# Root-mean-square normalisation in the second block: the gain applied in its own pass, and all eight tiles of squares summed by TensorE

## What is computed

```python
def rms_norm_2(x, g, eps=1e-6):
    xf = x.astype(jnp.float32)
    y = xf * lax.rsqrt(jnp.mean(xf * xf, axis=-1, keepdims=True) + eps)
    return (y * g.astype(jnp.float32)).astype(x.dtype)

for i in range(DEPTH):                                                   # DEPTH = 2
    h = x + 0.5 * swiglu_2(rms_norm_2(x, norm_ffn1[i]), ...)             # which = 0
    u = rms_norm_2(h, norm_mix[i])                                       # which = 1
    ...                                   # u @ w_in, attention, convolution, gates, w_o
    h = h + 0.5 * swiglu_2(rms_norm_2(h, norm_ffn2[i]), ...)             # which = 2
    x = h + (p[i] @ w_pe_proj[i]) * sigmoid(rms_norm_2(h, norm_pe[i]) @ w_pe_gate[i])   # which = 3
```

## Time and profile before

| | |
|---|---|
| median of 3 runs | 2408.21 us (2407.85 to 2410.92) |
| the profiled execution, its own time | 2407.85 us |
| its span in the trace | 2406.0 us |
| TensorE (PE) busy | 2281.4 us, 95% |
| VectorE (DVE) busy | 1648.2 us, 69% |
| ScalarE (ACT) busy | 1174.0 us, 49% |
| GpSimd (POOL) busy | 183.2 us, 8% |

### The profile page before, as it was taken

One profiled execution on the slowest core, in us unless ns is written; L12 is line 12 of the kernel. 1 busy time (PEld: TensorE's weight loads), 2 busy tenths in 40 slices (PEclk: granted clock), 3 DMA queues, 4 the chain that ended last, 5 costly groups with the idle time before them and its releaser, 6 DMA issues.

```text
span 2406.0 us, 40710 instructions
## 1 busy us (share of the span) xinstructions
PE 2281.4 (95%) x16812; PEld 2151.2 (89%) x16812; DVE 1648.2 (69%) x1717; ACT 1174.0 (49%) x1198; POOL 183.2 (8%) x185
## 2 busy tenths in 40 slices
PE   4999889999999998999899999999999999999999
PEld 4997788799889877899799997899999999889999
DVE  5886786786589876855655569865565546986555
ACT  2443555454354445454354455555355536465534
POOL 0110000010001100000012000012001200001200
PEclk9999999999999999999999999999999999999999
DMA  8996433576569752555545542445544554334453
GB/s 343 350 353 223 152 140 110 211 302 260 192 231 355 304 201 88 187 199 175 183 172 178 183 165 108 140 175 178 189 180 157 182 185 158 112 138 181 182 180 140
DMA packets 75937, 471.55 MB, mean 196 GB/s; under 512 B 8707, under 2 KB 8963, under 8 KB 27580
## 3 DMA queue, kind: packets, MB, share of 16 engines
q1 hardware_dynamic: 53136, 383.80, 43.6%
q0 software_dynamic: 18976, 68.71, 7.6%
q10 hardware_dynamic: 3724, 17.56, 2.0%
HBM read 468.97 MB, written 1.06 MB: 195 GB/s over the span
## 4 chain that ended last, share of the span: by engine, by line
PE 75%; DVE 12%; ACT 6%; DMA 4%; issue 2%; ACTq 0%; DVEq 0%; SPq 0%
PE ab L1736 48%; PE acc L1736 13%; PE acc L1856 8%; DVE wlo L964 3%; ACT whi L417 2%; DMA raw<-stream 2%; DVE sc L1559 1%; PE mb L2078 1%; DMA modmem<-mods 1%; DMA par<-params 1%; PE mb L1907 1%; DVE sc L1049 1%; DVE rstd L1161 1%; DVE x L1159 1%; DVE sc L1157 1%
## 5 line engine op out<-in xcount | busy, mean ns | idle before, releaser
L1736 PE MATMUL ab<-u_hi,whi 128*128 128x256 f32 x3664 | 1051.3, 287 | 33.8 <-DVE wlo L964 11.5
L964 DVE TENSOR_TENSOR wlo<-raw,whi 128x2048 fp32r<-128x2048 f32 x361 | 825.0, 2287 | 320.0 <-ACT whi L417 318.2
L1736 PE MATMUL ab<-u_lo,whi 128*128 128x256 f32 x3664 | 1042.3, 284 | 0.0
L1736 PE MATMUL ab<-u_hi,wlo 128*128 128x256 f32 x3664 | 1041.9, 284 | 0.0
L417 ACT ACTIVATE whi<-raw 128x2048 fp32r<-128x2048 f32 x361 | 688.9, 1910 | 536.7 <-DMA raw<-stream 339.2
L1736 PEld LDWEIGHTS ab<-u_hi,whi 128*128 128x128 f32 x3664 | 708.8, 193 | 49.7 <-issue 30.7
L1736 PEld LDWEIGHTS ab<-u_lo,whi 128*128 128x128 f32 x3664 | 709.1, 194 | 0.4
L1736 PEld LDWEIGHTS ab<-u_hi,wlo 128*128 128x128 f32 x3664 | 708.7, 193 | 0.0
L1736 PE MATMUL acc<-h_hi,whi 128*128 128x256 f32 (+1 forms) x1032 | 293.4, 284 | 6.9 <-DVE sc L1620 3.5
L1736 PE MATMUL acc<-h_lo,whi 128*128 128x256 f32 (+1 forms) x1032 | 292.0, 283 | 0.0
L1736 PE MATMUL acc<-h_hi,wlo 128*128 128x256 f32 (+1 forms) x1032 | 292.0, 283 | 0.0
(11 more groups left out here) (319 smaller groups left out, 2004.1 us busy)
## 6 DMA issues: line engine op xcount, KB each, us to landing
raw<-stream SPq DMA_DIRECT2D x365, 1024.0 KB, 4.8
modmem<-mods POOLq DMA_DIRECT2D x128, 512.0 KB, 6.1
sc<-lnrows ACTq DMA_DIRECT2D x5, 1024.0 KB, 4.9
sc<-start ACTq DMA_DIRECT2D x4, 1024.0 KB, 16.6
gateb<-gaterows ACTq DMA_DIRECT2D x6, 512.0 KB, 4.1
hank<-toep POOLq DMA_DIRECT2D x8, 192.0 KB, 4.0
x<-xT ACTq DMA_DIRECT2D x1, 1024.0 KB, 31.6
x<-xn ACTq DMA_DIRECT2D x1, 1024.0 KB, 5.0
```

Source lines behind the costliest of these rows:

```text
L964: nc.vector.tensor_tensor(wlo[:, n % RAW, :], raw[:, n % RAW, :], whi[:, n % RAW, :].bitcast(F32), ALU.subtract).then_inc(lo_ready, 1)
L1736: ins = nc.tensor.matmul(out, l, r, start=first and i == 0, stop=last and i == 2, skip_group_check=True)
```

## The change

It is made in `norm2` and `squares` only.
- ScalarE now writes x times gain in float32 into tiles `UF` to `UF+7` of `sc` (two instructions for each pair, semaphore `xg_ready`), and then `u_hi` from there by one copy of the pair (`lead`, which waits for `xg_ready`). For `which` 1 to 3 the copy of a pair follows its gain at once; for `which` 0 it follows the gain of the next pair. The four squares come after the last copy.
- ScalarE's `catch_up` stands ahead of pair 1 for `which` 1 to 3, ahead of everything for (1,0), and there is none for (0,0). In the code before it stood behind the first `lead` in all joins but (0,0).
- VectorE makes `u_lo` by `u_lo_pairs`, one subtraction for each pair. `sum_squares` is gone, with its semaphore.
- TensorE's `squares` takes all 8 tiles of squares, with a wait for `sq_ready` for each pair, by 8 float32 matmuls in place of 2.

```diff
@@ scalar: norm2
                 def lead(q):
+                    act.wait_ge(xg_ready, cnt["uf"] + q + 1)
+                    nc.scalar.activation(u_hi[:, 2 * q:2 * q + 2, :], sc[:, UF + 2 * q:UF + 2 * q + 2, :],
+                                         ACT.Copy).then_inc(uhi_ready, 1)
+
+                if (l, which) == (1, 0):
+                    catch_up()
+                for q in range(4):
+                    if which and q == 1:
+                        catch_up()
                     act.wait_ge(x_ready, cnt["x"] + q + 1)
                     for m in (2 * q, 2 * q + 1):
-                        ins = nc.scalar.activation(u_hi[:, m, :], x[:, m, :], ACT.Copy, scale=par[:, gc + m:gc + m + 1])
-                    ins.then_inc(uhi_ready, 1)
-
-                def square(q):
+                        ins = nc.scalar.activation(sc[:, UF + m, :], x[:, m, :], ACT.Copy,
+                                                   scale=par[:, gc + m:gc + m + 1])
+                    ins.then_inc(xg_ready, 1)
+                    if which:
+                        lead(q)
+                    elif q:
+                        lead(q - 1)
+                if not which:
+                    lead(3)
+                cnt["uf"] += 4
+                cnt["x"] += 4
+                for q in range(4):
                     nc.scalar.activation(sc[:, Z + 2 * q:Z + 2 * q + 2, :], x[:, 2 * q:2 * q + 2, :],
                                          ACT.Square).then_inc(sq_ready, 1)
-
-                lead(0)
-                if (l, which) != (0, 0):
-                    catch_up()
-                lead(1)
-                square(0)
-                square(1)
-                lead(2)
-                square(2)
-                lead(3)
-                square(3)
-                cnt["x"] += 4
                 cnt["var"] += 1
@@ vector: norm2
-                def rest(q):
-                    cnt["uhi"] += 1
-                    dve.wait_ge(uhi_ready, cnt["uhi"])
-                    for m in (2 * q, 2 * q + 1):
-                        ins = nc.vector.scalar_tensor_tensor(out=u_lo[:, m, :], in0=x[:, m, :], scalar=par[:, gc + m:gc + m + 1],
-                                                             in1=u_hi[:, m, :].bitcast(F32), op0=ALU.mult, op1=ALU.subtract)
-                    ins.then_inc(u_ready, 1)
-
-                def sum_squares(q):
-                    dve.wait_ge(sq_ready, cnt["sq"] + q + 1)
-                    ins = nc.vector.tensor_tensor(sc[:, Z:Z + 2, :], sc[:, Z:Z + 2, :], sc[:, Z + 2 * q:Z + 2 * q + 2, :], ALU.add)
-                    ...
-                update(0)
-                if which:
-                    rest(0)
-                    update(1)
-                    catch_up()
-                    rest(1)
-                    update(2)
-                    rest(2)
-                    update(3)
-                    sum_squares(1)
-                    sum_squares(2)
-                    rest(3)
-                else:
-                    ...
-                sum_squares(3)
+                for q in range(4):
                     if scale is not None:
                         x_update(q, scale, add)
+                    if which and q == 1:
+                        catch_up()
+                    if which:
+                        u_lo_pairs(q)
+                    elif q:
+                        u_lo_pairs(q - 1)
+                if not which:
+                    u_lo_pairs(3)
                     if scale is not None:
                         catch_up()
@@ tensor
+            def sums(src, tiles, ready, base, out, per=2, done=None):
+
+                for m in range(tiles):
+                    pe.wait_ge(ready, base + m // per + 1)
+                    ins = nc.tensor.matmul(out, meanones, src[:, m, :], start=(m == 0), stop=(m == tiles - 1))
+                ins.then_inc(done, 1)
+
             def squares():
 
-                cnt["sq"] += 1
-                pe.wait_ge(sqsum_ready, cnt["sq"])
-                for m in range(2):
-                    ins = nc.tensor.matmul(mb[:, 1, 0:T], meanones, sc[:, Z + m, :], start=(m == 0), stop=(m == 1))
-                ins.then_inc(var_ready, 1)
+                sums(sc[:, Z:Z + 8, :], DM, sq_ready, cnt["sq"], mb[:, 1, 0:T], 2, var_ready)
+                cnt["sq"] += 4
```

More of the change, by code:

```diff
@@ L218, in build @@
         sq_ready = sem("sq_ready")
-        sqsum_ready = sem("sqsum_ready")
         var_ready = sem("var_ready")
@@ L224, in build @@
         x_ready = sem("x_ready")
+        xg_ready = sem("xg_ready")
         rinv_ready = sem("rinv_ready")
@@ L951, in _ @@
             ph = [0]
-            cnt = {"std": 0, "uhi": 0, "sq": 0, "h": 0, "hhi": 0, "g2": 0, "sig": 0, "row": 0, "gate0": 0, "gate1": 0}
+            cnt = {"std": 0, "uhi": 0, "h": 0, "hhi": 0, "g2": 0, "sig": 0, "row": 0, "gate0": 0, "gate1": 0}
             def link(ins):
@@ L1210, in norm2 @@
             def norm2(l, which, scale=None, add=None):
-                gc = AT["norms2"][0] + 16 * which + 8 * l
-                def update(q):
+                for q in range(4):
                     if scale is not None:
                         x_update(q, scale, add)
-                def rest(q):
-                    cnt["uhi"] += 1
-                    dve.wait_ge(uhi_ready, cnt["uhi"])
-                    for m in (2 * q, 2 * q + 1):
-                        ins = nc.vector.scalar_tensor_tensor(out=u_lo[:, m, :], in0=x[:, m, :], scalar=par[:, gc + m:gc + m + 1],
-                                                             in1=u_hi[:, m, :].bitcast(F32), op0=ALU.mult, op1=ALU.subtract)
-                    ins.then_inc(u_ready, 1)
-                def sum_squares(q):
-                    dve.wait_ge(sq_ready, cnt["sq"] + q + 1)
-                    ins = nc.vector.tensor_tensor(sc[:, Z:Z + 2, :], sc[:, Z:Z + 2, :], sc[:, Z + 2 * q:Z + 2 * q + 2, :], ALU.add)
-                    if q < 3:
-                        link(ins)
-                    else:
-                        ins.then_inc(sqsum_ready, 1)
-                update(0)
-                if which:
-                    rest(0)
-                    update(1)
-                    catch_up()
-                    rest(1)
-                    update(2)
-                    rest(2)
-                    update(3)
-                    sum_squares(1)
-                    sum_squares(2)
-                    rest(3)
[L1246 to L1253, removed]
+                    if which and q == 1:
[6 more added lines that the diff above has]
+                    u_lo_pairs(3)
                     if scale is not None:
                         catch_up()
-                    sum_squares(1)
-                    sum_squares(2)
-                sum_squares(3)
-                cnt["sq"] += 4
                 cnt["std"] += 1
```

## The result

The changed kernel is slower: a median of 2440.20 us (2436.96 to 2441.81, 4 runs) against 2408.03 us (2406.84 to 2410.92, 4 runs), ratio 1.013 with a 95% interval of 1.0112 to 1.0148. The forecast had been 2434, 2427 to 2439: the direction was right, the size 6 us short and just outside the range. The profiled execution took 2437.39 us (span 2435.6), 29.5 more than that of before. So of the 6 us 3.4 show in the trace, and 2.8 are the distance from the profiled execution to the median.

A forecast was written before the change was run, and what follows sets the result against it. PE was taken as the bound, busy for 95% of the span and carrying 75% of the chain that ended last. 20.7 + 4.8 - 0.2 + 0.9 = +26.2 us on 2407.85 gave 2434 us, range 2427 to 2439.

The forecast's parts named there:

- Twelve more records, 2.59 us a join, all on PE's path: PE's squares in all eight joins: 16 records instead of 4, 0.216 us each, nothing hidden, +20.7 us in all.
- The last pair late by 0.8 us in six joins: Ordinary joins: PE stalls for pair 3's u_lo before its first block's last 12 matmuls, 0.8 us each, +4.8 us.
- The squares no wait, the removed sums worth nothing: In (0,1), ScalarE's squares end at 1398.0, PE arrives at 1398.1; VectorE's saved 3 x 0.69 us a join gains nothing.
- (0,0), 2.4: Join (0,0): one 0.69 us subtraction replaces two L1222 (0.88 us) before PE starts, -0.2 us beside the 2.59 of passes.
- (1,0), "I take +0.9 us": Join (1,0): allowance beyond the passes, since PE idles more and the clock may fall again; +0.9 us, bounds 0 and +4.5.
- about 0.65 us that the half clock cost the next block isn't lost: Behind squares in (1,0): the next block no longer runs at half clock, so about 0.65 us is taken back.
- Downstream: After squares: later waits and PE's next block move together with the last record; nothing given back, nothing more lost.
- "Nothing more is lost" downstream: After the joins: no further time added; the attention stretches were forecast at 0 in both layers.
- VectorE as the bound: Rival for the joins: VectorE's savings give 22.6 us back and hide PE's passes, 2385 us; chance 2%.
- cheap passes: Rival for squares: a record costs only 0.12 us, first term 11.5 us, total 2425; chance 3%.
- absorption downstream: Rival: PE's later waits for VectorE's convolution taps absorb the (.,1) joins' extra 3.4 us in each layer, 2427; chance 7%.
- The slower clock: Rival: in (1,0) or at a new stall, one or two more 1.2 GHz stretches on dense work, 2437 to 2442; chance 12%.

The follow-up runs named there:

- TensorE's part alone: Kernel before with squares summing all 8 tiles by 8 float32 matmuls and VectorE's sums gone, u_hi and u_lo made as before: 2424.49 us, ratio 1.0071.
- the first trace: First profiled execution of the changed kernel, set against the first profiled execution of the kernel before: 2437.39 us.
- the other two: Second and third traces of the changed kernel, run again unaltered: second with a median of 2436.14 us (4 runs), third 2436.90 us.
- The second comparison: Changed kernel, unaltered, timed against the kernel before on another occasion: median 2436.14 us (4 runs), ratio 1.0115.
- the first two experiments: Kernel before with 8 float32 matmuls and no VectorE sums: 2424.49 us; kernel before with one more VectorE addition and 1 matmul for 2: 2406.71 us.

## Why the prediction was right, and where it failed

- **Twelve more records, 2.59 us a join, all on PE's path:** shown. TensorE's part alone costs 2.59 in each ordinary join, 2424.49 us in all against 2425 expected, and halving the records gives 0.43 back.
- **The last pair late by 0.8 us in six joins:** shown. PE's new distance is 0.70 to 0.86 us in the first trace (0.67 to 0.98 in the other two), 12 matmuls ahead of squares, and the joins cost 0.67 to 0.83 beyond the passes; the sum is 20.05 us against 20.3 forecast. The chain of gain, copy and subtraction, read from the kernel's start, fitted to 0.1 us.
- **The squares no wait, the removed sums worth nothing:** both as forecast, L1924 having no idle time.
- **(0,0), 2.4:** measured 2.26, 2.57 and 2.44.
- **(1,0), "I take +0.9 us":** this term failed, in two parts. The three starts were right, and so was the statement that the clock might fall. But 5.76 us came in place of 3.5. First, the half clock: the forecast put 0.9 on top of its path, a mean over "may fall", where three traces have it fall each time, at 2.4 to 2.6 us, 2.3 of it ahead of squares. Second, "about 0.65 us that the half clock cost the next block isn't lost": PE waits there for VectorE's weight remainder and the path costs 3.2 at full clock, not 2.56. The forecast's "Downstream" had said itself that nothing is given back. The rows to see the first part by were there. After 1.21 busy us of 3.40 the clock had fallen in this very join, and the forecast's own path had PE idle for the first 3.8 us, then at work for 1.4 of every 3.5. The Trainium skill ("TensorE: Matmul & The Clock Gate", HAM oscillation) describes the same for short groups of matmuls between waits for DMA: after each wait the next group starts at the low level. The trace agrees in kind, for waits on VectorE, with 0.50 granted on all of the 13.7 us.
- **"Nothing more is lost" downstream:** 1.9 us were counted in the attention stretches. The kernel before shows 1.0 of it between two of its own executions, so part of it may be the reference and not the change. This stays open.
- **What the parts add up to** in the joins of the first trace: passes 17.5, the late pair 4.5, the order of the copies in (1,0) with its half clock 6.3, (0,0) -0.2; 28.1 of 29.6.
- **The range** was made from the terms' bounds and left out the spread of the executions themselves, 2434.4 to 2441.8 for the changed kernel. The second comparison (+27.3 us) would have lain within it, the first (+32.2) didn't.
- **Rivals:** VectorE as the bound and cheap passes fell with the first two experiments, and absorption downstream didn't occur. The slower clock, at 12%, is what happened in (1,0), and its 2437 to 2442 holds the median; that the median lies as high as 2440 is luck in part, since 2.8 us of it aren't in the trace.

## What to carry to other kernels

Where TensorE carries the path, an addition on an engine that has slack at that moment (0.42 us hidden) beats a plain float32 matmul (0.43 us in full). An engine that frees up gives nothing back unless somebody was waiting for it. Where PE is fed in small portions, look for the order in which each portion is ready earliest, and count a fall of the granted clock as the likeliest event, not as a risk: in join (1,0) the copies placed behind the next pair's gain cost 6.3 us. Time won by a faster block is won only up to the next hand-over: here 0.57 us ended in a wait for VectorE. And before reading 2 us out of a difference between two traces, trace the same program twice.

## What was new about the hardware

Thirty useless matmul records in PE's waits made a join 2.4 to 2.6 us faster, since they kept the granted clock at 1.00 where it was 0.50 for 13.7 us. While PE waited for each pair that half clock cost nothing; it cost where 24 matmuls ran without a wait. And with no change in the program, the stretches of half clock fall differently: the two traces of the kernel before are 5.9 us apart on the way to the joins (the same matmul at 908.62 and at 902.72 us), and 0.6 us at the end.
